# Down products of a mixture-of-experts pass placed inside the next pass, on one core

## The reference

```python
def expert_block(args):
    xblk, e = args
    h = jax.nn.silu(xblk @ w_gate[e]) * (xblk @ w_up[e])     # 1024 -> 512, twice
    return h @ w_down[e]                                     # 512 -> 1024
yb = lax.map(expert_block, (xb, block_expert)).reshape(rows, d)
y = jnp.zeros((t, d), yb.dtype).at[buf_tok].add(yb * buf_gate[:, None], mode='drop')
...
x = layer_norm(ALPHA * x + moe_out, ln2_g[l], ln2_b[l])
```

## Time and profile before

| what | value |
|---|---|
| median of 3 runs | 1116.33 us (1115.43 to 1117.3) |
| time of the profiled execution | 1114.33 us |
| its span, first to last instruction | 1112.6 us |
| mean granted TensorE clock | 0.977 |
| busy: PE, PEld, DVE, ACT, POOL | 89%, 41%, 42%, 26%, 19% of the span |
| expert stage | from about 627 us to the end |
| chain that ended last | PE 51%, DMA 18%, DVE 16%, issue 8%, POOL 3% |

### The profile page before, as it was taken

One profiled execution on the slowest core, in us unless ns is written; L12 is line 12 of the kernel. 1 busy time (PEld: TensorE's weight loads), 2 busy tenths in 40 slices (PEclk: granted clock), 3 DMA queues, 4 the chain that ended last, 5 costly groups with the idle time before them and its releaser, 6 DMA issues.

```text
span 1112.6 us, 16547 instructions
## 1 busy us (share of the span) xinstructions
PE 989.5 (89%) x6068; PEld 456.1 (41%) x6069; DVE 472.8 (42%) x1006; ACT 283.9 (26%) x464; POOL 208.9 (19%) x331
## 2 busy tenths in 40 slices
PE   7999999999999999999993588888888888888785
PEld 3644465466457447444453222322222222222221
DVE  0695542563463363422436143433333333333333
ACT  1123322312322232200001133333333333333232
POOL 3000010010010010033000123333333333333332
PEclk9999999999999999999995699999999999999998
DMA  9332211210320220473709599899999999999992
GB/s 285 109 85 66 60 37 39 76 39 21 75 58 22 57 57 2 159 285 147 303 33 402 186 418 415 334 412 416 416 416 416 415 415 417 415 416 416 417 388 81
DMA packets 93855, 256.68 MB, mean 231 GB/s; under 512 B 15444, under 2 KB 60500, under 8 KB 68976
## 3 DMA queue, kind: packets, MB, share of 16 engines
q1 hardware_dynamic: 81904, 240.54, 56.2%
q0 software_dynamic: 11104, 13.29, 3.5%
q10 hardware_dynamic: 800, 2.15, 0.5%
HBM read 260.90 MB, written 21.23 MB: 254 GB/s over the span
## 4 chain that ended last, share of the span: by engine, by line
PE 51%; DMA 18%; DVE 16%; issue 8%; POOL 3%; ACT 1%; POOLq 1%; SPq 0%; DVEq 0%; ACTq 0%
DMA const<-y_rows,raw 18%; PE proj L1267 11%; PE proj L1226 11%; PE proj L1447 5%; PE bank L1357 5%; PE bank L1435 5%; POOL out L564 3%; DVE raw L1176 2%; PE bank L1520 2%; DVE raw L1161 2%; DVE raw L1158 2%; PE proj L1234 1%; PE proj L1245 1%; DVE arena L897 1%; DVE raw L1172 1%
## 5 line engine op out<-in xcount | busy, mean ns | idle before, releaser
L1267 PE MATMUL proj<-xT_sb,ring 128*128 128x512 f32 x384 | 182.1, 607 | 0.0
L1520 PE MATMUL bank<-arena 128*64 128x512 f32 x544 | 123.7, 596 | 11.0 <-PE bank L1540 11.0
L1226 PE MATMUL proj<-xT_sb,ring 128*128 128x512 f32 (+1 forms) x272 | 119.1, 594 | 0.0
L1158 DVE TENSOR_TENSOR raw<-bank,const 128x512 f32<-128x512 f32 x33 | 22.8, 692 | 196.6 <-DMA const<-y_rows,raw 196.5
L1267 PEld LDWEIGHTS proj<-xT_sb,ring 128*128 128x128 f32 x384 | 68.3, 189 | 68.3 <-issue 64.8
L1226 PEld LDWEIGHTS proj<-xT_sb,ring 128*128 128x128 f32 (+1 forms) x272 | 50.7, 188 | 64.6 <-issue 64.5
L1520 PEld LDWEIGHTS bank<-arena 128*64 128x64 f32 x544 | 39.7, 137 | 80.5 <-issue 80.5
L564 POOL DMA_INDIRECT out<-raw x33 | 33.3, 1008 | 178.3 <-DVE raw L1176 165.1
L1520 PE MATMUL bank<-gates,arena 128*64 128x512 f32 x256 | 59.9, 611 | 6.7 <-PE bank L1540 4.9
L754 ACT ACTIVATE const<-bank,raw 128x512 f32<-128x512 f32 x33 | 22.7, 687 | 154.8 <-PE bank L1540 154.7
L1357 PEld LDWEIGHTS bank<-arena 64*64 64x64 f32 x1536 | 52.8, 134 | 18.2 <-ACT arena L702 9.1
(11 more groups left out here) (277 smaller groups left out, 1310.8 us busy)
## 6 DMA issues: line engine op xcount, KB each, us to landing
arena<-w_gu SPq DMA_DIRECT2D x64, 1024.0 KB
gates<-w_gu SPq DMA_DIRECT2D x32, 1024.0 KB
arena<-w_down SPq DMA_DIRECT2D x24, 1024.0 KB
ring<-w_in SPq DMA_DIRECT2D x42, 512.0 KB, 3.9
gates<-w_down SPq DMA_DIRECT2D x16, 1024.0 KB
branches<-w_down SPq DMA_DIRECT2D x16, 1024.0 KB
xT_sb<-w_gu SPq DMA_DIRECT2D x16, 1024.0 KB
ring<-w_gu SPq DMA_DIRECT2D x16, 1024.0 KB
```

The source lines that it names most:

```text
L1158: dve.tensor_tensor(x2, x_now[n], y_low, ADD).then_inc(s_base, 1)
L1226: ins = pe.matmul(proj[0:w, b, :], ring[:, slot, k, 0:w], xT_sb[:, k, :], start=(k == 0), stop=(k == KT - 1))
L1267: ins = pe.matmul(proj[:, gate_at["bank"], :], ring[:, gate_at["slot"], k, :], xT_sb[:, k, :], start=(k == 0), stop=(k == KT - 1))
L1520: ins = pe.matmul(bank[SLOTS * h:SLOTS * h + SLOTS, 0, :], xeT[:, k % 4, SLOTS * (k // 4):SLOTS * (k // 4) + SLOTS], gu[k // 2][:, k % 2, ...
```

## The change

The down products of a pass are taken out of its `one_pass` into a function `down`, which the next pass calls between its k tiles 1 and 2 (the third k tile follows it). The join of statistics moves from between k tiles 3 and 4 to between k tiles 5 and 6. The last pass's down products stand behind the loop. Since a pass must now know which pass came before it and in which weight set, `expert` has four copies of `one_pass` in place of two, and the first four experts stand ahead of the loop, which now runs seven times. The wait for `s_yp` at an expert's head is gone. Chunks 4 and 5 have a semaphore of their own, and SyncE loads chunk 0 of the next expert ahead of chunks 4 and 5 of this one. On ScalarE and VectorE the first two passes of those that come behind number 31 stand outside the loop, with the alternating bank of kept rows.

```diff
+            def reload_expert(e, b, last=False):
+                for c in (1, 2, 3):
+                    reload(e, b, c, s_used, e * 4 + (c + 1 - 4 * SETS))
+                if not last:
+                    reload(e + 1, (b + 1) % SETS, 0, s_used, e * 4 + (5 - 4 * SETS))
+                for c in (4, 5):
+                    reload(e, b, c, s_useddown, e * 2 + (c - 3 - 2 * SETS))
...
-            with act.If(more > 0):
-                with act.Fori(0, more) as i:
+            for n in range(2):
+                with act.If(more > n):
+                    one_pass(N_EXP + n, n)
+            with act.If(more > 2):
+                with act.Fori(2, more) as i:
                     one_pass(i + N_EXP, None)
...
+            def down(p, b, loads, release):
+                pe.wait_ge(s_hT, p + 1)
+                pe.wait_ge(s_ye, p + 1)
...
-            def one_pass(p, b, loads, last):
+            def one_pass(p, b, loads, last, before):
...
                 for k in range(KT):
-                    if k == 4:
+                    if k == 2 and before:
+                        down(before[0], *before[1:])
+                    if k == 6:
                         pair_stats(p)
...
-            def expert(e, b, loads):
+            def expert(e, b, loads, first_of_all=False):
                 extra = pe.value_load(extra_i[0:1, bass.ds(e, 1)], min_val=0, max_val=MORE)
                 first = pe.value_load(first_i[0:1, bass.ds(e, 1)], min_val=0, max_val=PASSES - 2)
-                pe.wait_ge(s_yp, first + 1)
-                pe.sem_inc(s_used, 1)
+                earlier = () if first_of_all else (first - 1, (b - 1) % SETS, loads if b else loads - 16, True)
                 with pe.If(extra > 0):
-                    with pe.Fori(0, extra) as n:
-                        one_pass(first + n, b, loads, False)
-                one_pass(first + extra, b, loads, True)
-
-            with pe.Fori(0, N_EXP // SETS) as i:
+                    one_pass(first, b, loads, False, earlier)
+                    with pe.If(extra > 1):
+                        with pe.Fori(1, extra) as n:
+                            one_pass(first + n, b, loads, False, (first + n - 1, b, loads, False))
+                    one_pass(first + extra, b, loads, True, (first + extra - 1, b, loads, False))
+                with pe.If(extra < 1):
+                    one_pass(first, b, loads, True, earlier)
+
+            for b in range(SETS):
+                expert(b, b, 16, first_of_all=b == 0)
+            with pe.Fori(1, N_EXP // SETS) as i:
...
+            down(more + (N_EXP - 1), SETS - 1, 16 * (N_EXP // SETS), False)
             pair_stats(more + N_EXP)
```

More of the change, by code:

```diff
@@ L368, in program @@
         s_w = [[sem(f"w_in{b}_{c}") for c in range(NCH)] for b in range(SETS)]
-        s_used = sem("w_used")
+        s_used, s_useddown = sem("w_gate_up_used"), sem("w_down_used")
         s_idx, s_xe, s_xe0 = sem("index_ready"), sem("tokens_in"), sem("tokens_zeroed")
@@ L453, in _, with reload @@
                                  rows[:, at:at + T].partition_broadcast(SLOTS).rearrange("p a d -> p (a d)")).then_inc(s_lnback, 16)
[L455 to L463, removed]
+            def reload(e, b, c, used_by, count):
+                sp.wait_ge(used_by, count)
+                n = c * CHUNK
+                src = w_gu[bass.ds(e, 1), :, n:n + CHUNK] if n < GU else w_down[bass.ds(e, 1), :, n - GU:n - GU + CHUNK]
+                sp.dma_start(w_chunk[b][c], src.rearrange("a p n -> (a p) n")).then_inc(s_w[b][c], 16)
+            def reload_expert(e, b, last=False):
[5 more added lines that the diff above has]
+                    reload(e, b, c, s_useddown, e * 2 + (c - 3 - 2 * SETS))
+            reload(SETS, 0, 0, s_used, 1)
+            with sp.Fori(1, N_EXP // SETS - 1) as i:
                 for b in range(SETS):
-                    reload(sp.snap(i * SETS + b, min_val=0, max_val=N_EXP - 1), b, i * (SETS * NCH) + (b - SETS) * NCH)
+                    reload_expert(sp.snap(i * SETS + b, min_val=SETS, max_val=N_EXP - SETS - 1), b)
+            for b in range(SETS):
+                reload_expert(N_EXP - SETS + b, b, last=b == SETS - 1)
         @block.gpsimd
@@ L1198, in _ @@
             more = dve.value_load(more_i[0:1, 0:1], min_val=0, max_val=MORE)
-            with dve.If(more > 0):
-                with dve.Fori(0, more) as i:
+            for n in range(2):
+                with dve.If(more > n):
+                    products(N_EXP + n)
+                    finish(N_EXP + n, n)
+            with dve.If(more > 2):
+                with dve.Fori(2, more) as i:
                     products(i + N_EXP)
@@ L1508, in pair_stats @@
                 ins.then_inc(s_pair, 1)
-            def one_pass(p, b, loads, last):
+            def down(p, b, loads, release):
+                pe.wait_ge(s_hT, p + 1)
+                pe.wait_ge(s_ye, p + 1)
+                wd = [v.rearrange("p (f h n) -> p f h n", f=2, h=2) for v in w_chunk[b][4:6]]
+                for f in range(4):
+                    if f % 2 == 0:
+                        pe.wait_ge(s_w[b][4 + f // 2], loads)
+                    for h in range(2):
+                        ins = pe.matmul(bank[SLOTS * h:SLOTS * h + SLOTS, 1, :], hT[:, f % 2, SLOTS * (f // 2):SLOTS * (f // 2) + SLOTS],
+                                        wd[f // 2][:, f % 2, h, :], start=(f == 0), stop=(f == 3))
+                    if f == 1 and release:
+                        ins.then_inc(s_useddown, 1)
+                ins.then_inc(s_yp, 1)
+            def one_pass(p, b, loads, last, before):
                 pe.wait_ge(s_xeT, p + 1)
@@ L1521, in one_pass @@
                                         gu[k // 2][:, k % 2, h, :], start=(k == 0), stop=(k == KT - 1))
+                        if k == 2 and h == 0 and before and before[-1]:
+                            ins.then_inc(s_useddown, 1)
                     if k == KT - 1:
@@ L1532, in one_pass @@
                     pe.sem_inc(s_used, 1)
[L1533 to L1544, removed]
             turn(0)
```

## The result

The changed kernel takes **1368.68 us** (median of 4 runs, 1367.18 to 1372.44) against 1115.88 (1114.47 to 1117.3) before: a ratio of **1.2274**, 95% interval 1.2246 to 1.2302. The forecast was 1125, the range 1116 to 1190. The direction was right, the size not by far.

The account below looks back on a forecast made before the run. The prediction took the gather loop, 14.22 us a pass, as the bound. Start +1.9, scatter +7.8 and end -1.1 made +8.6 us on the profiled 1114.33, 1122.9; with that execution 2.0 below the median, 1125 us, range 1116 to 1190.

Parts of the forecast that it names:

- The gather loop: Join, output scatter, gather of `y_low`, VectorE's wait, next join: claimed to bound a pass at 14.22 us without slack.
- TensorE's own loop: TensorE alone, join to join in the changed kernel: 14.27 us, as long as the gather loop, gain 0.0 a pass.
- this head in the sum: TensorE at an expert's start, from the `h` transposes to k tile 0, register loads and branch: 2.15 us.
- The rival that carried the fetch: TensorE's grown code must be fetched at leaps, stalling its sequencer: some 1150 us, or near 1190; chance 0.35.
- Seven first leaps: Fetch stalls at TensorE's first leaps alone, 1.8 to 5.5 us each: 13 to 38 us, some 1150; chance 0.14.
- five for each four experts: Further fetches if TensorE's loop isn't kept: 30 more, 37 x 1.8 = +67 us, near 1190; chance 0.21.
- the low price: 1.8 us for one TensorE instruction fetch, taken from a gather without weights in flight.
- The upper bound of 5.5: 5.5 us for one TensorE instruction fetch, taken from a gather with weights in flight.
- the sum's own 8.6: Start, scatter and end together: 1.9 + 7.8 - 1.1 = +8.6 us on the profiled 1114.33.
- The scatter of `y_e` late: Scatter lands 0.65 us late for the next pass's gather of `y_low`: 0.3 a pass over 26, +7.8 us.
- Start +1.9: Join of the second pass comes at 648.9 in place of 646.98: +1.9 us, once.
- End -1.1: Last pass: L1161 can start near 1101.6 in place of 1102.72, as `y_e` needs the down products alone: -1.1 us.

Follow-up runs that it names:

- e9: Kernel before, with GpSimd copying the next `y_low` gather's index column while it would wait for `x2`: 1110.5 us.
- e8: e5 with the numbers of the next turn's first expert also read early and kept in registers over the back edge: 1120.7 us.
- e3: Changed kernel's order with only two copies of a pass per expert and a short leap of some 125 instructions: 1153.4 us.
- e1: Kernel before, its order of work kept, with the changed kernel's layout: four pass copies per expert, first four experts ahead of the loop: 1340.4 us.
- e12: e8 with two more, never run, pass copies behind the branch of every expert in the loop (2022 instructions): 1267.3 us.
- e4: Kernel before with eight experts per turn of TensorE's loop in place of four, some 2060 instructions: 1149.1 us.
- e5: e3 with TensorE reading the next expert's two numbers during the current pass, for three of four experts: 1129.5 us.
- e10: e8 with the GpSimd index-copy edit of e9: 1114.1 us.
- e7: e4 with an instruction at the loop's head that announces the back edge's target: 1141.2 us.

## Why the prediction was wrong, point by point

- **The gather loop is bound at 14.22 us: right.** e9 shortened it and passes followed; e8 left it alone and stayed at 14.22, the mean of 18 passes, against 14.23 before.
- **TensorE's own loop, 14.27 us, gain 0: right for code at hand and at the full clock.** From the start of the `h` transposes to k tile 0 the sum had 2.15 us; e3's clean pass took 2.16, and 14.47 from join to join.
- **The step that failed is this head in the sum: its 2.15 us had nothing in them for bringing the code.** In the changed kernel it took 8.57 us in the pass shown above (825.49 to 834.06). The fetch was left to a rival, on the ground that the old loop was kept and its branches cost 0.2 us. The new one, of twice that length, is not kept, and the 36 stops took 185 us.
- **The rival that carried the fetch was what happened. Its count was right and its price was the second step to fail.** "Seven first leaps" and "five for each four experts" make 37 stops; 36 came. "The weights no longer fill the queue, the low price holds: 37 x 1.8" was wrong twice over. At 21 of the 29 long branches the DMA engines moved 254 to 423 GB/s, since the average of 267 hides that they stand idle at other times. And where they moved 8 to 33, a branch took 3.4 to 4.1 us: the 1.8 was the landing of a gather, and no row was one of a fetch. The upper bound of 5.5, taken 37 times, would have given +204, and with the sum's own 8.6 some 40 short of the 253; the range should have reached there.
- **The clock hung a second price on each stop and on the new gap, and was in no case of the forecast.** In the changed kernel the matmuls took 58.5 us longer. In e3, without stops, the gap of 1.7 us that the sum reckoned cost 1.7 us of clock in every second pass or so. Its matmuls took 18.5 us longer in all, and taking the gap away gave back 33 of its 38 us (e8).
- **The scatter of `y_e` late, +0.3 a pass: right in e3**, where the gather starts 3.23 us behind the end of `x2` (median), not 2.89 as in before. With the head shortened (e8) it is in time, 2.88.
- **Start +1.9:** the second join came at 648.23 in e3 (648.9 reckoned), in the changed kernel 7.6 us later, behind its first stop.
- **End -1.1: wrong in sign.** e8's last pass took 13.86 us against 12.09. Its down products ran at half clock there, 5.35 us where before's took 3.65, which is nearly all of the difference; and the 1.1 us didn't come either, as they began 5.9 us behind the join and not 5.0.
- **The chance.** The case had 0.35, with 0.21 for the loop that isn't kept. For it stood the length of the loop against what was fetched once, against it only that a loop half as long was kept; 0.35 was low for that, and this is a judgement behind the result.

## What to carry to other kernels

Count the instructions of a loop in the built program before copying its body into branches: here a loop of 1528 ran from what was fetched once, one of 2002 paid five stops a turn from its second turn on, nearly all of 3.4 to 6.7 us. Look for such stops behind the branch too, as "issue" ahead of a matmul, and not only at it. Price a new gap on TensorE at the clock it may cost, not only at its length: 1.7 us of waiting made the matmuls behind it cost 1.7 us more in every second pass. And ask of each engine's small steps on the closing chain whether they can be done while it waits: one index copy moved gained 5 us where the whole reordering, freed of its stalls, lost 5.

## What the runs showed of the hardware

- A taken branch in a loop that isn't kept: 5.3 to 7.7 us where the DMA engines moved 314 to 423 GB/s (one at 254 took 6.0), 4.2 to 4.9 at 250 to 301 (e1), 3.4 to 4.1 at 8 to 56. In a kept loop 0.2.
- In loops of 1990 to 2022 instructions leaps of 367 to 374 stop TensorE in one of two places: at the branch (all in e1 from the second turn on, three of four in a turn of the changed kernel), or some matmuls behind it, where the branch itself took 0.35 us (the fourth, and three in a turn of e12). Leaps of 123 in a loop of 2060 did neither (e4). Why one place or the other, no run says.
- In e3 and e5 the granted clock fell to half for 3.4 to 6.8 us behind a gap of 0.8 and one of 1.7 to 2.4 us with 0.44 us of transposes between, in somewhat over half of the passes. Behind stops of 7.2 to 12.0 us in the changed kernel it fell each time, for 6.8 to 13.7 us. In the steady passes of before and e8, with waits up to 1.6 us at the join and 0.9 us elsewhere, it stayed at 1.00; in e10 it fell four times behind gaps of 0.75 to 0.93.
- An announced branch (e7) took 0.47 us once and 5.1 and 5.3 us the other two times.
